# Scores of the first layer as three products of 64 rows, with two maps or heads in the two halves of the array's rows

## The reference, cut to what matters

```python
# (A) four differential heads, each with two maps of 64 features
s = einsum('bqhmd,bkhmd->bhmqk', qb, ka) * 64 ** -0.5 - slope * dist
p = softmax(where(visible, s, -inf)); w = p[:, :, 0] - lam * p[:, :, 1]
# (B) eight stick-breaking heads of 64 features
z = einsum('bqhd,bkhd->bhqk', qb, ks) * 64 ** -0.5
log_skip = where(earlier, log_sigmoid(-z), 0)
log_pass = cumsum(log_skip, reverse=True) - log_skip
a = where(earlier, exp(log_sigmoid(z) + log_pass), 0)
```

## Time and profile before

| | us |
|---|---|
| median of 3 runs (1375.06 to 1375.91) | 1375.52 |
| the profiled execution's own time | 1375.03 |
| its span in the trace | 1373.2 |
| PE busy | 1319.9 (96%) |
| DVE busy | 876.7 (64%) |
| ACT busy | 547.6 (40%) |
| POOL busy | 488.4 (36%) |

### The profile page before, as it was taken

How to read it: one execution, slowest core, us unless ns; L and a number is a source line. 1 busy time by engine, 2 the same in 40 slices (tenths; PEclk the granted TensorE clock), 3 DMA queues, 4 the chain that set the end, 5 groups by cost and what they waited for, 6 DMA issues and landing times.

```text
span 1373.2 us, 22469 instructions
## 1 busy us (share of the span) xinstructions
PE 1319.9 (96%) x8400; PEld 1242.5 (90%) x8400; DVE 876.7 (64%) x1973; ACT 547.6 (40%) x1290; POOL 488.4 (36%) x465
## 2 busy tenths in 40 slices
PE   8999999999899999997999999998999999999997
PEld 8999999999799999996888999998998989989886
DVE  5776869595587847668465323554767667677465
ACT  3443546463545535355111011533445445446200
POOL 3323232223234232347333323563433234335431
PEclk9999999999999999998999999999999999999999
DMA  6000111001011011113133211222111112106141
GB/s 221 32 32 31 47 32 47 16 31 47 32 39 40 22 42 51 59 41 123 58 122 133 94 46 38 86 81 70 40 47 39 47 36 71 57 20 199 61 163 76
DMA packets 47355, 88.26 MB, mean 64 GB/s; under 512 B 4480, under 2 KB 30080, under 8 KB 47120
## 3 DMA queue, kind: packets, MB, share of 16 engines
q1 hardware_dynamic: 44800, 78.45, 17.4%
q10 hardware_dynamic: 2448, 8.39, 1.6%
HBM read 66.84 MB, written 19.98 MB: 63 GB/s over the span
## 4 chain that ended last, share of the span: by engine, by line
PE 51%; DVE 4%; issue 2%; ACT 2%; POOL 2%; DVEq 0%; ACTq 0%; POOLq 0%
PE bank L1965 20%; PE bank L2109 13%; PE bank L2033 7%; PE bank L2083 5%; PE bank L2053 4%; DVE pb L1745 1%; ACT rtmp L1355 1%; PE bank L2004 1%; PE bank L2131 1%; POOL wsp L1046 1%; POOL pb L1235 0%; DVE ring L1760 0%; POOL big L1089 0%; DVE qpe L1621 0%; DVE qpe L1625 0%
## 5 line engine op out<-in xcount | busy, mean ns | idle before, releaser
L1965 PE MATMUL bank<-big,wsp 128*128 128x344 f32 (+2 forms) x3024 | 557.9, 328 | 6.4 <-DVE big L1562 3.3
L1965 PEld LDWEIGHTS bank<-big,wsp 128*128 128x128 f32 x3024 | 480.6, 189 | 10.2 <-POOL wsp L1046 4.7
L1045 POOL TENSOR_SCALAR wsp<-wraw 128x1024 fp32r<-128x1024 f32 (+3 forms) x92 | 83.6, 908 | 538.6 <-PE bank L1965 418.3
L1760 DVE TENSOR_TENSOR ring<-bank,ring 128x256 fp32r<-128x256 f32 (+3 forms) x292 | 156.5, 553 | 82.8 <-ACT ring L1437 79.9
L1437 ACT ACTIVATE ring<-bank 128x256 fp32r<-128x256 f32 (+3 forms) x292 | 138.7, 495 | 149.5 <-PE bank L2053 107.4
L2109 PE MATMUL bank<-big,wsp 128*128 128x512 f32 x816 | 195.9, 398 | 0.0
L1046 POOL TENSOR_TENSOR wsp<-wraw,wsp 128x1024 fp32r<-128x1024 f32 (+3 forms) x92 | 186.6, 2028 | 7.7
L2083 PE MATMUL bank<-ring,vtok 128*128 128x256 f32 (+2 forms) x1276 | 183.2, 281 | 2.3 <-DVE ot L1772 1.2
L2109 PEld LDWEIGHTS bank<-big,wsp 128*128 128x128 f32 x816 | 152.9, 189 | 34.8 <-DVE big L1799 0.4
L2083 PEld LDWEIGHTS bank<-ring,vtok 128*128 128x128 f32 (+1 forms) x1276 | 171.8, 191 | 7.9 <-issue 4.0
L1965 PE MATMUL bank<-h1t,wsp 128*128 128x344 f32 (+2 forms) x1080 | 173.8, 322 | 1.5 <-DVE lraw L1610 1.5
(11 more groups left out here) (133 smaller groups left out, 1435.7 us busy)
## 6 DMA issues: line engine op xcount, KB each, us to landing
wraw<-in_w SPq DMA_DIRECT2D x47, 512.0 KB, 3.5
wraw<-y_scratch SPq DMA_DIRECT2D x17, 448.0 KB, 3.7
woraw<-in_wo SPq DMA_DIRECT2D x12, 512.0 KB, 4.9
y_scratch<-ot SPq DMA_DIRECT2D x40, 128.0 KB, 1.7
xres<-in_x SPq DMA_DIRECT2D x8, 512.0 KB, 4.6
h_scratch<-res ACTq DMA_DIRECT2D x8, 512.0 KB, 2.7
gate_scratch<-gtmp SPq DMA_DIRECT2D x8, 512.0 KB, 2.9
gate<-gate_scratch SPq DMA_DIRECT2D x8, 512.0 KB, 3.6
```

Source lines behind the costliest of these rows:

```text
L1045: pool.wait_ge(S["pool_step"], tick(nc.gpsimd.tensor_scalar(hi, raw, 1.0, 1.0, ALU.mult, ALU.mult)))
L1760: V.tensor_tensor(R[0:rows, r % NRING, 1, 0:w], bank[T_BANK[t]][0:rows, 0:w], lo_hi(R[0:rows, r % NRING, 0, 0:w]), ALU.subtract).then_inc( ...
L1965: ins = mm(dst, wsp[:, SLOT[kind, u], a, k, :], rhs[:, b, k0 + k, c0:c0 + w], start=(k == 0 and a == 0 and b == 0), stop=last)
```

## The change

Queries and keys of the first layer stay as projected: 128 rows with map or head 0 in rows 0 to 63 and 1 in rows 64 to 127, hi in slice 0 and lo in slice 1, in two buffers for units in turn. ScalarE and VectorE each evacuate a piece in one instruction of 128 rows; GpSimd copies nothing in the first layer. A score step makes two chunks at once, of the two maps of an A head or of the two heads of a B unit: six matmuls of 64 rows, in turn in the upper and the lower half of the array's rows, into two banks. The second map's or head's own step is left with nothing to do. Scores are ordered chunk by chunk with the maps (or heads) in turn; VectorE's scans stay in the order of the heads. In the planner a pair costs `pe_ns(w) * 3 + 400`, and q0 follows the scores of the unit before the last.

```diff
 def score_steps(g):
-    return [("S", t, m, c) for t in GROUP_STEPS[g] for m in range(maps_of(GROUPS[g][1]))
-            for c in range(len(score_chunks(TSTEPS[t][1])))]
+    return [("S", t, m, c) for t in GROUP_STEPS[g] for c in range(len(score_chunks(TSTEPS[t][1])))
+            for m in range(maps_of(GROUPS[g][1]))]
+def score_order(groups):
...
+        if GROUPS[g][1] == "B":
+            if GROUPS[g][3] == 0:
+                out += between(score_steps(g), score_steps(g + 1))
...
-            after += [("pool", copied)] if copied in within else []
-            after += [evacuated(("P", "qn", u, cq))] if layer else []
-        L.put("pe", "S", s, pe_ns(w) * (5 if layer else 2), after, 170)
+            after += [("pool", copied)] if layer and copied in within else []
+            after += [evacuated(("P", "qn" if layer else "q0", u, cq))]
+        if layer:
+            L.put("pe", "S", s, pe_ns(w) * 5, after, 170)
+        elif is_first(s):
+            after += [freed(s_steps[n - 2])] if n >= 2 else []
+            L.put("pe", "S", s, pe_ns(w) * 3 + 400, after, 170)
+        else:
+            L.put("pe", "S", s, 0, [], 170)
...
-                L.put("dve", "C", ("C", t), 2.45 * n_all + 50, [("act", s), emptied(g)], 90)
+                scans[t] = 2.45 * n_all + 50, [("act", s), emptied(g)]
+    for t in sorted(scans):
+        L.put("dve", "C", ("C", t), *scans[t], 90)
...
-            if kind in ("q0", "qn", "qr") and u >= 1:
+            if kind in ("qn", "qr") and u >= 1:
                 end = [last_score(u - 1, c)]
+            if kind == "q0" and u >= 2:
+                end = [last_score(u - 2, c)]
...
-                    for m in range(2):
-                        ins = A(qst[0:64, m, 0, cc], src[64 * m:64 * m + 64, 0:w], ACT.Copy, scale=q_scale(u))
+                    ins = A(qst[:, u % 2, 0, cc], src[:, 0:w], ACT.Copy, scale=q_scale(u))
...
-                    for m in range(2):
-                        ins = V.tensor_tensor(kst[64:128, u % 2, m, cc], src[64 * m:64 * m + 64, 0:w],
-                                              lo_hi(kst[0:64, u % 2, m, cc]), ALU.subtract)
+                    ins = V.tensor_tensor(kst[:, u % 2, 1, cc], src[:, 0:w], lo_hi(kst[:, u % 2, 0, cc]), ALU.subtract)
...
-                    j = m if kind == "A" else head
-                    prods = [(qst[:, j, a, qc], kst[:, u % 2, j, c0:c0 + w]) for a in (0, 1)]
-                for k, (l, r) in enumerate(prods):
-                    ins = mm(dst, l, r, start=(k == 0), stop=(k == len(prods) - 1))
-                ins.then_inc(S["s_done"], 1)
+                    halves = [slice(64 * j, 64 * j + 64) for j in range(2)]
+                    prods = [(b, qst[h, u % 2, a, qc], kst[h, u % 2, b_, kc])
+                             for a, b_ in ((0, 0), (0, 1), (1, 0)) for b, h in zip(mine, halves)]
+                for k, (b, l, r) in enumerate(prods):
+                    ins = mm(bank[S_BANK[b]][:, 0:w], l, r, start=(k < len(mine)), stop=(k >= len(prods) - len(mine)))
+                    if k >= len(prods) - len(mine):
+                        ins.then_inc(S["s_done"], 1)
```

More of the change, by code:

```diff
@@ L173, in score_steps, with pair_of, is_first @@
 def score_steps(g):
-    return [("S", t, m, c) for t in GROUP_STEPS[g] for m in range(maps_of(GROUPS[g][1]))
-            for c in range(len(score_chunks(TSTEPS[t][1])))]
+    return [("S", t, m, c) for t in GROUP_STEPS[g] for c in range(len(score_chunks(TSTEPS[t][1])))
+            for m in range(maps_of(GROUPS[g][1]))]
+def score_order(groups):
+    out = []
+    for g in groups:
+        if GROUPS[g][1] == "B":
+            if GROUPS[g][3] == 0:
+                out += between(score_steps(g), score_steps(g + 1))
+        else:
+            out += score_steps(g)
+    return out
+def pair_of(s):
+    _, t, m, c = s
+    other = t + len(GROUPS[TSTEPS[t][0]][4])
+    return [("S", t, 0, c), ("S", t, 1, c)] if kind_of(t) == "A" else [("S", t, 0, c), ("S", other, 0, c)]
+def is_first(s):
+    return s[2] == 0 if kind_of(s[1]) == "A" else GROUPS[TSTEPS[s[1]][0]][3] == 0
 def queries(u, chunks):
@@ L326, in weave @@
     groups = [g for u in units for g in unit_groups(layer, u)]
-    s_steps = [s for g in groups for s in score_steps(g)]
+    s_steps = score_order(groups)
     within = WITHIN[layer]
@@ L330, in weave @@
     t0 = s_steps[0][1]
+    scans = {}
     def last_score(u, c):
@@ L363, in weave @@
             cq = chunk_of(i)
[L364 to L367 removed]
+            copied = ("P", "qr", u - u % 2, cq)
+            after += [("pool", copied)] if layer and copied in within else []
[5 more added lines that the diff above has]
+            L.put("pe", "S", s, pe_ns(w) * 3 + 400, after, 170)
+        else:
+            L.put("pe", "S", s, 0, [], 170)
         if kind == "B":
@@ L540, in weave @@
         if kind in ("q0", "qr"):
-            L.put("pool", "Q", s, 1400 if kind == "q0" else 900, [("dve", s)], 70)
+            if kind == "qr":
+                L.put("pool", "Q", s, 900, [("dve", s)], 70)
         if kind in ("v0", "vn") and c == 2:
@@ L634, in count_before @@
     return out
-Q_COPY = count_before(PROJ, lambda s: s[1] in ("q0", "qr"))
+Q_COPY = count_before(PROJ, lambda s: s[1] == "qr")
 ROTATED = count_before(PROJ, lambda s: s[1] in ("kpe", "qr"))
@@ L1140, in copy_queries @@
                 for m in range(2):
-                    if kind == "q0":
-                        to, from_ = qst[64:128, m, :, cc], qst[0:64, m, :, cc]
-                    elif m == 0:
+                    if m == 0:
                         to, from_ = qpe[64:128, m, 0, cc], qpe[0:64, m, 0, cc]
@@ L1209, in _ @@
                         clear_meta_values(1)
-                if s[0] == "P" and s[1] in ("q0", "qr"):
+                if s[0] == "P" and s[1] == "qr":
                     copy_queries(s)
@@ L1585, in evacuate @@
                 if kind == "k0":
-                    for m in range(2):
-                        ins = V.tensor_tensor(kst[64:128, u % 2, m, cc], src[64 * m:64 * m + 64, 0:w],
-                                              lo_hi(kst[0:64, u % 2, m, cc]), ALU.subtract)
+                    ins = V.tensor_tensor(kst[:, u % 2, 1, cc], src[:, 0:w], lo_hi(kst[:, u % 2, 0, cc]), ALU.subtract)
                 elif kind == "q0":
[L1590 to L1593, removed]
+                    ins = V.scalar_tensor_tensor(out=qst[:, u % 2, 1, cc], in0=src[:, 0:w], scalar=q_scale(u),
+                                                 in1=lo_hi(qst[:, u % 2, 0, cc]), op0=ALU.mult, op1=ALU.subtract)
                 elif kind in ("v0", "vn"):
@@ L2007, in scores @@
             def scores(t, m, c):
+                s = ("S", t, m, c)
                 g, i, slot = TSTEPS[t]
                 layer, kind, u, head, _ = GROUPS[g]
+                if layer == 0 and not is_first(s):
+                    return
                 q0, rows = query_cols(i)
-                chunks = score_chunks(i)
-                c0, w = chunks[c]
+                c0, w = score_chunks(i)[c]
                 if m == 0 and c == 0 and head == 0:
                     cq = chunk_of(i)
+                    pe.wait_ge(S["proj_evac"], EVAC_AT["P", "qn" if layer else "q0", u, cq])
@@ L2016, in scores @@
                     if layer:
[L2017 to L2023, removed]
+                        pe.wait_ge(S["q_copied"], Q_COPY["P", "qr", u - u % 2, cq])
@@ L2024, in scores @@
+                if t == FIRST_C:
+                    pe.wait_ge(S["hide_rows"], 2)
+                mine = [S_CHUNK[x[1:]] for x in ([s] if layer else pair_of(s))]
+                for b in mine:
+                    if S_BEFORE[b] is not None:
+                        pe.wait_ge(S["s_free_" + S_OWNER[S_BEFORE[b]]], S_FREED[S_BEFORE[b]])
+                qc, kc = slice(q0, q0 + 128), slice(c0, c0 + w)
                 if kind == "C":
-                    if t == FIRST_C:
-                        pe.wait_ge(S["hide_rows"], 2)
```

8 lines of the change are left out of this document (4 added, 4 removed).

## The result

The changed kernel takes 1387.33 us, the median of four runs (1386.85 to 1388.04), against 1375.29 in the same comparison: a ratio of 1.0088 (95% interval 1.0076 to 1.0100). That is 12.0 us slower. The forecast was 19.7 slower, with a range of 1371 to 1427.

What follows compares the result with a forecast made beforehand. PE, busy 96% of the span, was taken to bound the kernel. From 1375.03 us, +46.8 for excursions, -18.7 for three waves and -8.2 for sooner queries gave 1394.9, forecast as 1395, range 1371 to 1427.

Steps and rivals of the forecast that it cites:

- Part 1: First-layer score matmuls on PE: a pair's halves stream side by side, three waves for four matmuls, -18.7 us.
- rival 1: Weight loads of score pairs: the two halves' loads go one after the other, +27.6 us, 1422; chance 0.2.
- rival 4: Score pairs on PE: streams of the two halves do not overlap, +56 us, 1451; chance 0.04.
- Part 2: PE going to 64 rows and back around each of 120 pairs: 0.39 us each, +46.8 us.
- Part 3: Queries before a unit's first scores: shorter chain and two buffers remove PE's waits on GpSimd's copy, -8.2 us.
- Part 4: Fewer evacuations and copies on ACT, DVE and POOL: covered by PE, nothing; new two-bank wait nothing, 0 to 6.
- Rival 5: Score banks: pairs wait for two of three, 0.05 to 0.1 us a pair, 1401 to 1407; chance 0.05.
- the forecast's own case: Whole kernel: 1383 (excursion of 0.28 to 0.3 us) to 1402 (0.43), centre 1395; chance 0.49.

Runs made afterwards that it cites:

- experiment 4: Kernel before, with GpSimd's copy of the queries made for unit 0 alone, later scores waiting for VectorE's evacuation: 1364.29 us (ratio 0.9927).
- 9: Changed kernel with four matmuls of 128 rows a pair, queries and keys evacuated in two instructions of 64 rows, order replanned: 1373.01 us (ratio 0.9991).
- 6: Changed kernel with four matmuls of 128 rows a pair in place of six of 64, all engines' order replanned for them: 1358.47 us (ratio 0.9888).
- experiment 2: Changed kernel with all six matmuls of a pair in the upper 64 rows of the array: 1436.26 us (ratio 1.0462).
- experiment 5: Kernel before, with one matmul in 120 of 240 chunks reading only rows 0 to 63, adding 120 excursions: 1415.27 us (ratio 1.0297).
- experiment 1: Changed kernel with four matmuls of 128 rows a pair in place of six of 64, order not replanned: 1370.56 us (ratio 0.9969).
- experiment 3: Changed kernel with the queries of a unit projected as late as with one buffer: 1387.41 us (ratio 1.0092).
- 11: Changed kernel with queries and keys evacuated in two instructions of 64 rows each, planner told: 1400.36 us (ratio 1.0185).
- experiment 7: Changed kernel with four score banks and one turn bank in the first layer, pairs made two by two, 60 excursions: 1458.6 us (ratio 1.0613).

## Why the forecast came out

The steps from the kernel before to the changed one, each between two measured forms:

| step | from, to (us) | measured | forecast |
|---|---|---|---|
| no copy of the queries (experiment 4) | 1374.6, 1364.3 | -10.3 | -8.2 |
| pairs on two of three banks, order of chunks and scans, second buffer (4 to 9) | 1364.3, 1373.0 | +8.7 | 0 (0 to 6) |
| one evacuation instruction (9 to 6) | 1373.0, 1358.5 | -14.5 | 0 |
| three waves and 120 excursions (6 to the change) | 1358.5, 1387.3 | +28.8 | +28.1 |
| sum | | +12.7 | +19.9 |

The first row has the kernel before as measured beside the experiments; in the result's own comparison the change was +12.0 and the forecast +19.7.

**Part 1, three waves for four matmuls (-18.7): right.** Loads and streams go two by two; rival 1 (serial loads, 1422) and rival 4 fall. The distances in the trace show the loads, experiment 2 the streams. The Trainium skill, "TensorE: Matmul & The Clock Gate", Part 3: Packing small matmuls — row/col tiling, What overlaps and what doesn't, has loads overlap matmuls in flight only where their row group differs; here loads of all 128 rows hide behind matmuls of all 128 rows throughout (PE busy 590.85 and PEld 566.01 of 609 us, starts 0.159 us apart), so for this kernel the measurement decides against it. The same part of that page of the Trainium skill says that matmuls in different row groups run concurrently, their starts at most 4 ns apart; the trace bears it out, with starts 3 to 6 ns apart in the median.

**Part 2, 0.39 us for each of 120 excursions (+46.8): right for PE.** The trace has 0.39 as the median; together with part 1 the kernel pays 28.8, forecast 28.1. That these agree to 0.7 us is partly luck: by the windows under experiment 9, 5.3 of the 28.6 us are more idle time of PE and only 23.3 more busy time; added alone, 120 excursions cost 40.5, 0.34 each, and 0.31 at an equal clock (experiment 5); and in an unfit order the net was 16.8 (experiment 1 against the change). The forecast took what is added to PE's stream as lost almost one for one. Experiments 2 and 5 gave 49 for 56 and 37 to 45 for 46.8, since PE waits less when it is slower. The step that made it right was to see that small matmuls hide the first load of an excursion and wide ones do not: the bare rows said 0.19 and 0.28. The Trainium skill, "TensorEngine Tiling (Array Packing)", Key Properties, has a change of tiling mode drain TensorE; the trace agrees for 64 rows as for 16, with the 0.39 us.

**Part 3, the queries sooner (-8.2): the right size, the wrong reason for part of it.** The second buffer gave nothing (experiment 3). The copy alone gave 10.3. In the changed kernel, as far as idle time of PE shows it, most of that went again to other waits: it fell by 1.7 us in all.

**Part 4, the lighter evacuation at nothing: wrong, and the term that made the forecast 7.7 us too high.** "PE covers all of it" was read from shares: DVE at 70% of the stage, ACT at 48%. It was 14.5 us in the form with four matmuls and 13.0 in the changed kernel. The shares say nothing of the places where PE has only work that waits for VectorE: a unit's last wide scores and the end of the last unit, where PE's waits are on the score reads and the split of turned weights. The forecast's window ended at 637 us and so left out a wait of 3.1 us for that split, at 645.7 us in the kernel before. Nor had it a price for the clock: about half of the 13 to 14.5 us is idle time of PE, and a third to a half, by the estimates under experiments 9 and 11, the clock of 1.2 GHz beside it. In the same part, the wait for two banks with the new order was put at 0 to 6 and is 8.7 with all that came along in that step; it was not split further, so how much is the banks and how much the order of chunks and scans is open. The two errors have opposite signs: -14.5 and +8.7 leave -5.8, and with the copy's -2.1 and parts 1 and 2 at +0.7 that is the -7.2 between the sums of the table. That a term off by 14.5 us moved the total by 7.7 is luck.

Rival 5 (pairs wait for banks, 1401 to 1407) has its mechanism in the trace, 5.8 us of waits on L1720, yet not its sum, since the evacuations paid for it. The upper edge of the forecast's own case, 1402, is 2 us more than its 0.43 us an excursion gives (1400); nothing hangs on it. The direction was earned by parts 1 and 2; the total lies well in the range with the help of errors that partly cancel.

## What to carry to other kernels

In this kernel a pair saves one stream of about 0.15 us and pays 0.39 for the two changes of mode, so halving the rows of its matmuls could pay only with more work in one excursion; no run here shows such a gain (experiment 7 lost it to other waits and to the clock). Count the changes of mode beside the columns. Work of an engine at 70% is not free in a program whose order is fixed: one instruction of 128 rows in place of two of 64 was worth 13 to 14.5 us, about half of it in waits of PE and much of the rest in the lower clock beside them. And an order planned with one cost is no fair test of work with another: the same matmuls took 1370.6 and 1358.5.

## What was not expected of the hardware

Weight loads into the two halves of the array start together, in pairs 0.11 us apart; a single load of 128 columns has that pace too. Two matmuls of 64 rows in different halves stream at the pace of one. In experiment 7, with 39 us of idle time on PE spread over the stage, the granted clock of that stage fell to 0.95, and by the estimate above that cost the kernel more than the idle time did.
